# Hybrid decoder trunk: router turned round, expert scatter by one-hot head and rest, first dense turn moved

## The reference

```python
def swiglu(x, w1, w3, w2):
    return (jax.nn.silu(x @ w1) * (x @ w3)) @ w2

def moe_ffn(x, w_router, w1, w3, w2):
    t = x.reshape(B * S, D)
    logits = (t @ w_router).astype(jnp.float32)
    top_val, top_idx = lax.top_k(logits, TOP_K)          # TOP_K = 2
    top_w = jax.nn.softmax(top_val, axis=-1)
    comb = jnp.sum(jax.nn.one_hot(top_idx, N_EXPERTS, dtype=jnp.float32) * top_w[..., None], axis=1)
    y = jnp.zeros_like(t)
    for e in range(N_EXPERTS):
        y = y + comb[:, e:e + 1] * swiglu(t, w1[e], w3[e], w2[e])
    return y.reshape(B, S, D)
```

## Time and profile before

| | us |
|---|---|
| median of 3 runs | 1674.03 (1673.22 to 1674.40) |
| the profiled execution, its own time | 1672.28 |
| its span, first to last instruction | 1670.50 |
| TensorE busy | 1609.2 |
| VectorE busy | 1281.5 |
| ScalarE busy | 1017.0 |
| one expert job, gather to gather | 124.89 |
| mean granted TensorE clock (1 is 2.4 GHz) | 0.988 |

### The profile page before, as it was taken

How to read it: one execution, slowest core, us unless ns; L and a number is a source line. 1 busy time by engine, 2 the same in 40 slices (tenths; PEclk the granted TensorE clock), 3 DMA queues, 4 the chain that set the end, 5 groups by cost and what they waited for, 6 DMA issues and landing times.

```text
span 1670.5 us, 20822 instructions
## 1 busy us (share of the span) xinstructions
PE 1609.2 (96%) x7640; PEld 1327.1 (79%) x7641; DVE 1281.5 (77%) x1274; ACT 1017.0 (61%) x931; POOL 52.0 (3%) x75
## 2 busy tenths in 40 slices
PE   7999989999999996999999999999999999999996
PEld 6887778888788775888888888888888888888884
DVE  5786664455777665888888888888888888888886
ACT  5557333433454623776776776776776776776773
POOL 0000000000000001000000000000000000000000
PEclk9999989999999998999999999999999999999998
DMA  9552356555546147699998998998998998998991
GB/s 328 175 183 70 102 175 202 191 187 184 169 142 209 51 152 253 219 371 316 372 372 313 374 371 312 374 373 312 375 372 311 376 370 313 375 368 315 363 382 66
DMA packets 230074, 452.59 MB, mean 271 GB/s; under 512 B 9856, under 2 KB 15488, under 8 KB 230016
## 3 DMA queue, kind: packets, MB, share of 16 engines
q1 hardware_dynamic: 226064, 447.57, 76.1%
q10 hardware_dynamic: 3952, 4.26, 0.9%
HBM read 450.75 MB, written 1.05 MB: 270 GB/s over the span
## 4 chain that ended last, share of the span: by engine, by line
PE 94%; DVE 4%; ACT 1%; issue 1%; DMA 1%; POOL 0%; DVEq 0%; SPq 0%; POOLq 0%; ACTq 0%
PE bank L1268 28%; PE bank L1270 28%; PE bank L1269 28%; PE bank L1640 4%; PE bank L1584 2%; PE bank L1572 2%; PE bank L1403 1%; ACT split L376 1%; DVE split L382 1%; DMA raw<-w_in_dram 1%; PE bank L1426 0%; DVE xT L815 0%; PE bank L1425 0%; PE bank L1424 0%; DVE x L1028 0%
## 5 line engine op out<-in xcount | busy, mean ns | idle before, releaser
L398 DVE TENSOR_TENSOR split<-raw,split 128x2048 fp32r<-128x2048 f32 x327 | 748.2, 2291 | 127.3 <-ACT split L393 126.9
L393 ACT CAST split<-raw 128x2048 fp32r<-128x2048 f32 x327 | 625.6, 1914 | 196.5 <-PE bank L1270 196.5
L1268 PE MATMUL bank<-split,xeT 128*128 128x512 f32 x896 | 357.1, 399 | 1.4 <-DVE xeT L815 1.4
L1270 PE MATMUL bank<-split,xeT 128*128 128x512 f32 x896 | 349.6, 390 | 0.0
L1269 PE MATMUL bank<-split,xeT 128*128 128x512 f32 x896 | 348.9, 389 | 0.0
L376 ACT CAST split<-raw 128x2048 fp32r<-128x2048 f32 (+3 forms) x97 | 176.4, 1818 | 255.9 <-PE bank L1270 254.1
L382 DVE TENSOR_TENSOR split<-raw,split 128x2048 fp32r<-128x2048 f32 (+3 forms) x97 | 210.9, 2177 | 154.5 <-ACT split L376 154.1
L1268 PE MATMUL bank<-split,xT 128*128 128x512 f32 (+2 forms) x544 | 212.8, 391 | 9.4 <-DVE xT L815 5.0
L1269 PE MATMUL bank<-split,xT 128*128 128x512 f32 (+2 forms) x544 | 210.3, 387 | 0.0
L1270 PE MATMUL bank<-split,xT 128*128 128x512 f32 (+2 forms) x544 | 210.2, 386 | 0.0
L1268 PEld LDWEIGHTS bank<-split,xeT 128*128 128x128 f32 x896 | 168.3, 188 | 36.5 <-issue 1.7
(11 more groups left out here) (224 smaller groups left out, 1344.6 us busy)
## 6 DMA issues: line engine op xcount, KB each, us to landing
raw<-moe_w_dram SPq DMA_DIRECT2D x330, 1024.0 KB, 5.8
raw<-w_in_dram SPq DMA_DIRECT2D x32, 1024.0 KB, 6.1
raw<-dense_w_dram SPq DMA_DIRECT2D x30, 1024.0 KB, 5.1
raw<-w_out_dram SPq DMA_DIRECT2D x8, 1024.0 KB, 5.0
early<-moe_w_dram SPq DMA_DIRECT2D x6, 1024.0 KB, 12.8
raw<-w_o_mla_dram SPq DMA_DIRECT2D x4, 1024.0 KB, 5.0
raw<-w_o_dsa_dram SPq DMA_DIRECT2D x4, 1024.0 KB, 5.1
raw<-w_in_dram SPq DMA_DIRECT2D x4, 912.0 KB, 4.8
```

The costliest lines, as they stand in the source:

```text
L393: act.copy(split[:, n % SPLIT, HEAD, :], landing(n, j)[:, :]).then_inc(heads_made, 1)
L398: dve.tensor_tensor(split[:, n % SPLIT, REST, :], landing(n, j)[:, :], split[:, n % SPLIT, HEAD, :].bitcast(F32), ALU.subtract).then_inc(r ...
L1268: pe.matmul(out_, act_[REST], w[HEAD], start=first, stop=False)
L1270: return pe.matmul(out_, act_[HEAD], w[REST], start=False, stop=last)
```

## The change

- **Dense.** The turn of the first group comes after the first half of w1 of the second group, and goes to banks 5 and 7 (`dense_turn_bank`), which w2 uses only later. That w1 now waits for `silu_ready` instead of `hidden_rest`. ScalarE and VectorE take their part of the turn one unit later.
- **Router.** Operands are swapped: the tokens are stationary, 8 columns of weights are streamed, and logits come out with tokens on partitions. The copy and the turn back go. The maxima are read from the bank.
- **Counts.** `sel` and the copies of `before` and `ones` (`counters`, two more copies on VectorE) are fp32r; five calls remain, of one entry each. The places' three signal first, the counts' two after.
- **Job 0's pick.** VectorE makes it at once, before the weights. `slot_no` counts from 1, so one step fewer. GpSimd's loop runs from 1.
- **Scatter.** `pick` itself is turned into `pickT` (fp32r). The result becomes head (ScalarE) and rest (VectorE, `expert_out_rest`, twice a job). A scatter is 8 fp32r calls. The sum on VectorE multiplies by the weight of each token.

```diff
         def one_hots(j, e, half):
...
-                pool.wait_ge(pick_put, j + 1)
-                pool.wait_ge(comb_tr, j + CREDIT)
-                for t in range(T):
-                    ins = pool.tensor_tensor(comb_at[:, t, :], pick[:, t, :], cur[:, 2 + t:3 + t].to_broadcast([P, CAP]), ALU.mult)
-                ins.then_inc(comb_put, 1)
-
-            pool.sem_inc(comb_put, CREDIT)
-            with pool.Fori(0, EXPERTS) as e:
+                pool.wait_ge(y_add, 4 * j + CREDIT)
+                pool.tensor_copy(cur[:, 2:4], r_comb[:, :, bass.ds(e, 1)].rearrange("p t n -> p (t n)")).then_inc(comb_put, 1)
+
+            with pool.Fori(1, EXPERTS) as e:
...
         def dve_experts(dve, step):
...
+            for i, ones_and in enumerate((before, ones)):
+                dve.tensor_copy(counters[:, i, :], ones_and[:, :]).then_inc(slot_ids, 1)
...
             dve.wait_ge(route_mm, 1)
-            dve.tensor_copy(logitsT[:, :], bank[6][0:EXPERTS, 0:SEQ]).then_inc(logits_ev, 1)
-            dve.wait_ge(logits_tr, 1)
+            for t in range(T):
+                dve.max(r_top[:, t, :], lg[:, t, :])
...
             step(dve.scalar_tensor_tensor(out=r_pos, in0=pos, scalar=1.0, in1=r_sel, op0=ALU.add, op1=ALU.mult))
-            step(dve.tensor_scalar(r_pos, r_pos, -1.0, None, ALU.add))
+            for t in range(T):
+                ins = dve.tensor_scalar(pick[:, t, :], slot_no[:, 0:CAP], r_pos[:, t, 0:1], None, ALU.is_equal)
+            ins.then_inc(pick_put, 1)
...
+            def expert_out_rest(j, h):
+                dve.wait_ge(oe_ev, 2 * j + (h + 1 + CREDIT))
+                at = slice(h * W, (h + 1) * W)
+                rest_of(dve, [oe[:, i, at] for i in (HEAD, REST)], bank[4 + h][:, :], oe_rest)
+
             def add_up(j):
...
-                        dve.tensor_tensor(y[:, t, h * W:(h + 1) * W], y[:, t, h * W:(h + 1) * W], bank[SCATTER[h][t]][:, :], ALU.add).then_inc(y_add, 1)
+                        at = slice(h * W, (h + 1) * W)
+                        dve.scalar_tensor_tensor(out=y[:, t, at], in0=bank[SCATTER[h][t]][:, :], scalar=cur[:, 2 + t:3 + t], in1=y[:, t, at],
+                                                 op0=ALU.mult, op1=ALU.add).then_inc(y_add, 1)
 
             def job(j, is_first):
                 if not is_first:
                     for m in range(2):
                         job_rest(dve, j, m)
+                        expert_out_rest(j - 1, m)
...
                     if g and kind == "w1" and half == 0:
-                        pe.wait_ge(h_rest, T * (g - 1) + t + 1)
+                        pe.wait_ge(h_rest if g > 1 else silu_ev, T * (g - 1) + t + 1)
...
-                    if (kind, g, half, t) == ("w3", 0, 1, T - 1):
+                    if (kind, g, half, t) == ("w1", 1, 0, T - 1):
                         turn(0)
...
-                    pe.matmul(out_, w[HEAD][:, i, :], x_i[REST], start=(i == 0), stop=False)
-                    pe.matmul(out_, w[REST][:, i, :], x_i[HEAD], start=False, stop=False)
-                    ins = pe.matmul(out_, w[HEAD][:, i, :], x_i[HEAD], start=False, stop=(i == KD - 1))
+                    x_i = x_at(i, t)
+                    pe.matmul(out_, x_i[REST], w[HEAD][:, i, :], start=(i == 0), stop=False)
+                    pe.matmul(out_, x_i[HEAD], w[REST][:, i, :], start=False, stop=False)
+                    ins = pe.matmul(out_, x_i[HEAD], w[HEAD][:, i, :], start=False, stop=(i == KD - 1))
...
                 for h in range(2):
-                    pe.wait_ge(oe_ev, 2 * j + (h + 1 + CREDIT))
-                    for t in range(T):
-                        pe.matmul(bank[SCATTER[h][t]][:, :], combT[:, t * P:(t + 1) * P], oe[:, h * W:(h + 1) * W],
-                                  start=True, stop=True).then_inc(sc_mm, 1)
+                    pe.wait_ge(oe_rest, 2 * j + (h + 1 + CREDIT))
+                    for t in range(T):
+                        to, slots = bank[SCATTER[h][t]][:, :], pickT[:, t * P:(t + 1) * P]
+                        pe.matmul(to, slots, oe[:, REST, h * W:(h + 1) * W], start=True, stop=False)
+                        pe.matmul(to, slots, oe[:, HEAD, h * W:(h + 1) * W], start=False, stop=True).then_inc(sc_mm, 1)
```

More of the change, by code:

```diff
@@ L230, in build @@
         r_list, r_top, r_keys = rt[:, :, 0:16], rt[:, :, 16:24], rt[:, :, 24:32]
-        r_sel, r_exp, r_comb, r_pos = (rt[:, :, 32 + 8 * i:40 + 8 * i] for i in range(4))
+        r_exp, r_comb, r_pos = (rt[:, :, 40 + 8 * i:48 + 8 * i] for i in range(3))
         r_one = rt[:, :, 72:76]
+        sel = put("sel", [P, T, EXPERTS], r_vm + 1024, F32R)
+        counters = put("counters", [P, 2, P], r_vm + 2048, F32R)
         cur = small[:, 160:164]
@@ L559, in hT_of, with dense_turn_bank @@
             return hT_odd if g % 2 else hT
+        def dense_turn_bank(g, t):
+            return bank[2 * t + (0 if g else 5)]
         def slots_of(g):
@@ L578, in turned @@
                     act.wait_ge(h_tr, T * g + t + 1)
-                    act.copy(hT_of(g)[:, HEAD, 0:k, t * P:(t + 1) * P], blocks(bank[2 * t], k)).then_inc(h_ev, 1)
+                    act.copy(hT_of(g)[:, HEAD, 0:k, t * P:(t + 1) * P], blocks(dense_turn_bank(g, t), k)).then_inc(h_ev, 1)
             for m, (kind, g, half) in enumerate(ffn_units(DG)):
@@ L585, in act_dense @@
                     turned(g + 1)
-                if (kind, g, half) == ("w3", 0, 1):
+                if (kind, g, half) == ("w1", 1, 0):
                     turned(0)
@@ L604, in expert_out @@
                 act.wait_ge(sc_mm, 4 * j + CREDIT)
-                act.copy(oe[:, h * W:(h + 1) * W], bank[4 + h][:, :]).then_inc(oe_ev, 1)
+                act.copy(oe[:, HEAD, h * W:(h + 1) * W], bank[4 + h][:, :]).then_inc(oe_ev, 1)
             def job(j, is_first):
@@ L637, in job @@
                         act.wait_ge(sc_mm, 4 * j + CREDIT)
-                        act.copy(combT[:, :], bank[7][:, 0:SEQ]).then_inc(comb_ev, 1)
+                        act.copy(pickT[:, :], bank[7][:, 0:SEQ]).then_inc(comb_ev, 1)
             act.sem_inc(comb_ev, CREDIT)
@@ L831, in turned @@
                     dve.wait_ge(h_ev, T * g + t + 1)
-                    rest_of(dve, [hT_of(g)[:, i, 0:k, t * P:(t + 1) * P] for i in (HEAD, REST)], blocks(bank[2 * t], k), h_rest)
+                    rest_of(dve, [hT_of(g)[:, i, 0:k, t * P:(t + 1) * P] for i in (HEAD, REST)], blocks(dense_turn_bank(g, t), k), h_rest)
             for m, (kind, g, half) in enumerate(ffn_units(DG)):
@@ L937, in dve_experts @@
             dve.sem_inc(y_add, CREDIT)
+            dve.sem_inc(oe_rest, CREDIT)
             extra = all_jobs(dve, job)
+            for h in range(2):
+                expert_out_rest(extra + (EXPERTS - 1), h)
             add_up(extra + (EXPERTS - 1))
```

72 lines of the change are left out of this document (34 added, 38 removed).

## The result

The changed kernel took 1665.32 us in the median of 20 executions, the kernel before 1672.36 us in the median of 20. By these medians the change is a gain of 0.4%. The ratio on record, 0.994 (0.992 to 0.9965), says 0.6%, because it counts the executions in the fast state alone and so leaves out the three longest of the changed kernel. The forecast was 1.4%, and the median lies outside the range of 1645 to 1657.5.

A forecast was written before the change was run, and what follows sets the result against it. TensorE, busy 96%, was taken as the bound. Gains of 5.2 + 6.0 + 11.1 + 0.9 = 23.2 us from 1672.28 gave 1649.1; 1.75 carried over to the median made 1650.8 us, range 1645 to 1657.5.

The forecast's parts named there:

- the sum: Total of the forecast gains, 5.2 + 6.0 + 11.1 + 0.9 = 23.2 us against the profiled execution of 1672.28 us.
- Dense turn: After the first dense group: moving the turn closes a 3.47 us gap and avoids half clock behind it; 5.2 us gained.
- lower end: Dense part: 3.0 us gained if the clock falls anyway or the other executions didn't have the fall.
- Router: Router to job 0's first product: swapped operands, fewer counting entries, pick on VectorE; 6.0 us gained, ends 1.6 and 8.7.
- The first rival: The clock falls in the router, whose part gains 1.6 to 2.5 us; 1654.5 to 1656 us, chance 0.15.
- signs of being wrong: TensorE waiting for split each job, sums over 0.69 us, clock 0.50 before the counts, router products 0.2 us apart.
- the end without the fall: Router part's upper end, with the clock not falling there: 8.7 us gained.
- Scatter: Expert jobs: eight calls at 0.227 us replace eight entries of 0.43; 1.62 us a job, 11.1 for seven in the loop.
- the second rival: Scatter's gain is given back in the loop because a weight remainder comes late; 1661.9 us, chance 0.12.
- the third: Rival: the four sums with a per-partition factor cost much more than 0.69 us; at 2.0 each 1681 us, chance 0.02.
- the fourth: Rival: scatter calls still go as two entries of 0.43 us each, 6.9 us a job; 1690 us, chance 0.02.
- End: After the last scatter: first sum starts 0.4 us earlier, then four sums on VectorE bound it; 0.9 us gained.

The follow-up runs named there:

- e1: Changed kernel with the first dense turn put back as in the kernel before; median 1657.40 us, ratio 0.9907, one of seven executions long at 1677.71.
- e2: Kernel before with only the first dense turn moved; six executions of 1663.92 to 1670.11 us, six of 1688.88 to 1690.10.
- e5: Kernel before with six repeated products ahead of w1 of the third dense group; eight executions of 1670.86 to 1677.34 us, four of 1695.21 to 1698.05.
- e4: Kernel before with four repeated products ahead of w1 of the third dense group; 1668.95 to 1677.38 us, ratio 1.0012.
- e11: Changed kernel with nine repeated products (2.04 us of waste) ahead of w1 of the third dense group; four executions of 1652.93 to 1654.03 us.
- e6: Kernel before with the moved dense turn and three small fp32 products in the wait ahead of the attention, both layers; 1664.93 to 1667.48 us, ratio 0.9971.
- e10: Kernel before with only three small fp32 products in the wait ahead of the attention, both layers; 1669.03 to 1673.55 us, ratio 0.9995.
- e7: e3 with the router's products, copy and turn back as in the kernel before; median 1646.53 us, ratio 0.9853.
- e8: e3 with job 0's pick and the copy of its weights' column moved from VectorE to GpSimd; median 1657.46 us, ratio 0.9916.
- e3: Changed kernel with three small fp32 products filling the wait ahead of the attention, both layers; median 1651.74 us, ratio 0.9879.

## Why the prediction was wrong

Point by point, by its own steps.

**The step that failed** is the one that is not in the sum: that outside the places the change touches, the clock stays as in the trace of before. "TensorE's granted clock was 1.00 (2.4 GHz) nearly everywhere" was read as a property of the kernel. The attention's start has a wait of TensorE, 1.42 us, and a few small products behind it, and it was no rival because it was neither touched nor slow. But its place in time was touched: everything ahead of it became 2 to 5 us shorter. In half of the executions the clock fell there and 20 us went. In the three long executions that were traced (after, e1, e2) the attention takes 58.1 to 58.2 us up to the output instead of 34.5, and 54.6 of them are at a clock of 0.50. The shown chain is: the long attention comes with the new turn (16 of 32) and hardly with the old one (2 of 82 unshifted); with the old turn shifted it comes in e5 (4 of 12) and not in e4 (0 of 12); it goes in every kernel in which the wait is filled (0 of 41). So the fall in the attention and the part of the wait in it are shown. Why an unfilled wait brings the fall in some executions and not in others stays open. The place in time is a reading and not more: e4's shift brought no long group, e11's took it away by another way than forecast, and the start of the first product doesn't sort the traces.

**Dense turn**, 5.2 forecast: the gap is gone, and no fall stands behind it in after. The 5.2 of the two traces agree with the forecast in part by luck. e6 against e10 gives 4.0 to 5.1; the short executions give less, 2.0 (after against e1's six, median 1657.26) and 3.1 (e2 against before). The prediction's lower end, 3.0, was meant for executions that don't have the fall, and e4's trace, with the old turn, is one: its clock is 1.00 from 240 to 260 us.

**Router**, 6.0 forecast: 2.9 measured, 24.99 against 22.12 us. The first rival, that the clock falls in the router, came true, and with it two of the prediction's own signs of being wrong, a clock of 0.50 before the counts and router products 0.2 apart. (Its time follows from its own terms as 1654.3 to 1655.2, not 1654.5 to 1656.) I had taken the value near the end without the fall "since in this trace the clock held through 631.97". That was one trace. With the 0.11 us products the clock fell 1.3 to 2.0 us behind the first of them in every trace; but with the 0.06 us ones, where it held for 5 to 9 us in five traces, it fell after 1.4 and 1.5 us in two (e6 and e5). So the turned products aren't shown to be its cause. Besides, I had the sizes of both kinds right, 0.11 and 0.215, and still wrote that the lost copy and turn back pay for them. They don't: e7, which keeps copy and turn back, passes this stage 3.7 us sooner. The router's real gain is the pick on VectorE, 5.6 us (27.74 in e8 against 22.11 in e3; 4.4 of them ahead of the gather, 1.2 from it to the first product, with the gather mostly at half clock), nearly all that I had reckoned for the stage. With the old products the stage gains 6.6 us, with the turned ones 2.9.

**Scatter**, 11.1 forecast: 11.1 measured from job 0's first product to the last scatter. The types of the weight products brought their pace, and neither the second rival (no wait in the junctions) nor the third (sums of 0.68) nor the fourth happened. **End**, 0.9: about 1.0.

With the attention at full clock the sum would have been 20.1 us instead of 23.2, and e3 shows it: 1651.74, 20.1 below the median of its comparison, 1671.85. So 20.1 of the 23.2 us were there, and the median still missed by 14.5 us. The changed kernel's own short executions reach 17.1 us, 3.5 less than e3; no trace was taken of one, and where these 3.5 us went is open. Last, the 1.75 us that the prediction carried over from the profiled execution to the median came from 3 executions; the median of 20 is 1672.36, 0.1 above the profiled one, so the sum should have ended at 1649.2.

The Trainium skill (TensorE: Matmul & The Clock Gate, section LDWEIGHTS) has a weight load cost by its columns, and its section on weight-path perf modes has a full load of a type other than FP32 twice as fast. The router rows decide for the first: with 128 columns loaded in fp32r and 8 streamed a product takes 0.11 us at full clock, and with 8 loaded and 128 streamed 0.06. At half clock they take 0.213 and 0.106, which the first section's single figure doesn't have.

## What to carry to other kernels

Look for waits of TensorE that stand just ahead of small products, wherever they are, and not only where the edit is: a change elsewhere in the program can bring on a fall of the clock behind such a wait, here for 20 us in half of the executions. Where one exists, fill it with a few small products; in e10 that cost nothing that could be measured (0.9995), and here it turned a two-valued time into one value. And compare the several executions before the median: two groups mean that one trace shows only one of them. When the operands of a small product can be swapped, keep the side with few columns stationary (0.06 us against 0.11 here).

## What I had not expected of the hardware

- The granted clock stayed at 0.50 for 54.6 us (545.33 to 599.95) with TensorE busy all the time. It did so for the same 54.6 us in e1 and e2 (547.27 to 601.89, 544.58 to 599.19), and in all three it was back 1.7 to 1.9 us before the first output product, still among the attention's small ones. In e11, fallen at the same place of the program, it was 0.50 only from 543.6 to 547.0. What sets these lengths isn't shown.
- The same program takes up to 3 us more or less to its second attention (548.66 and 545.69), by the short falls in the mixer and the dense part: from 20 us to the attention the mean clock was 0.98 in before and 0.99 in e1.
- Three fp32 products of 256 columns, the filler, are six entries and 1.46 us in e3; one fp32r product of 512 columns is a single entry of 0.23.
